# Two attention stages: the first tokens' output gated by halves, and ScalarE's high parts in another place

## What is computed

```python
q, k, v, f_logit, gate = _split(x @ w_in, [H * dh, H * dh, H * dh, H, D])
...
s = jnp.where(kpos[None, :] <= qpos[:, None], s, -jnp.inf)
p = jax.nn.softmax(s, axis=-1).astype(v.dtype)
return jnp.einsum('bhqs,bshd->bqhd', p, v)
...
return (jax.nn.silu(gate) * o.reshape(B, S, D)) @ w_out
```

## Time and profile before

| | us |
|---|---|
| median of 3 runs (1339.82 to 1340.50) | 1340.21 |
| the profiled execution's own time | 1334.75 |
| its span in the trace | 1333.0 |
| TensorE busy | 1280.7 (96%) |
| VectorE busy | 873.1 (65%) |
| ScalarE busy | 613.0 (46%) |
| TensorE's mean granted clock, share of full speed | 0.987 |

### The profile page before, as it was taken

The page is one execution under the profiler, slowest core; times in us unless marked ns, Lnnn a source line. Parts: engine busy times, 40 slices in busy tenths (PEclk is TensorE's granted clock), DMA queues, the critical chain, the costliest instruction groups (busy, mean ns, idle before and its releaser), DMA issues.

```text
span 1333.0 us, 16476 instructions
## 1 busy us (share of the span) xinstructions
PE 1280.7 (96%) x6717; PEld 1085.8 (81%) x6717; DVE 873.1 (65%) x1302; ACT 613.0 (46%) x838; POOL 24.1 (2%) x37
## 2 busy tenths in 40 slices
PE   6999999989999999999999988999999999999987
PEld 5888888978888888878888875778888899988876
DVE  6655557786655557685856668675555575667885
ACT  6444436525444445543544456554444443535361
POOL 2000000200000000000000000000000000000000
PEclk9999999999999999999999999999999999999899
DMA  9655545434655655456565340166555685346201
GB/s 305 223 189 184 186 152 181 160 127 143 205 189 189 189 190 172 155 179 222 188 198 181 102 158 1 46 207 190 189 190 169 118 234 165 130 163 217 96 1 63
DMA packets 158810, 218.16 MB, mean 164 GB/s; under 512 B 8256, under 2 KB 110992, under 8 KB 158736
## 3 DMA queue, kind: packets, MB, share of 16 engines
q1 hardware_dynamic: 156880, 212.56, 50.2%
q0 software_dynamic: 1376, 3.71, 0.9%
q10 hardware_dynamic: 480, 0.85, 0.2%
HBM read 216.04 MB, written 1.05 MB: 163 GB/s over the span
## 4 chain that ended last, share of the span: by engine, by line
PE 87%; DVE 7%; ACT 3%; issue 2%; DMA 1%; SPq 0%; DVEq 0%
PE PS L679 24%; PE PS L682 24%; PE PS L680 24%; PE PS L714 2%; PE PS L715 2%; PE PS L800 1%; ACT whi L1490 1%; PE PS L721 1%; DVE wlo L2010 1%; PE PS L992 1%; PE PS L699 1%; DMA raw<-in_ffn_w_in_dram 1%; PE PS L1275 1%; PE PS L1261 1%; PE PS L1288 1%
## 5 line engine op out<-in xcount | busy, mean ns | idle before, releaser
L2010 DVE TENSOR_TENSOR wlo<-raw,whi 128x2048 fp32r<-128x2048 f32 (+4 forms) x206 | 457.5, 2231 | 122.7 <-ACT whi L1490 121.9
L1490 ACT ACTIVATE whi<-raw 128x2048 fp32r<-128x2048 f32 (+4 forms) x206 | 381.4, 1864 | 64.4 <-DMA raw<-in_fox_w_in_dram 33.8
L679 PE MATMUL PS<-whi,XL 128*128 128x512 f32 (+3 forms) x992 | 385.4, 389 | 9.1 <-DVE XL L2057 3.5
L680 PE MATMUL PS<-wlo,XH 128*128 128x512 f32 (+3 forms) x992 | 379.3, 383 | 0.0
L682 PE MATMUL PS<-whi,XH 128*128 128x512 f32 (+3 forms) x992 | 264.6, 384 | 0.0
L679 PEld LDWEIGHTS PS<-whi,XL 128*128 128x128 f32 x992 | 187.1, 189 | 44.3 <-issue 3.9
L680 PEld LDWEIGHTS PS<-wlo,XH 128*128 128x128 f32 x992 | 187.2, 189 | 32.7
L682 PEld LDWEIGHTS PS<-whi,XH 128*128 128x128 f32 x992 | 185.1, 189 | 35.0
L1544 ACT ACTIVATE scr<-PS,rn 128x256 f32<-128x256 f32 x88 | 41.7, 474 | 227.0 <-PE PS L682 223.9
L679 PE MATMUL PS<-whi,GL 128*128 128x512 f32 x320 | 125.6, 392 | 0.0
L680 PE MATMUL PS<-wlo,GH 128*128 128x512 f32 x320 | 124.7, 390 | 0.0
(11 more groups left out here) (375 smaller groups left out, 1349.6 us busy)
## 6 DMA issues: line engine op xcount, KB each, us to landing
raw<-in_ffn_w_in_dram SPq DMA_DIRECT2D x174, 512.0 KB, 5.0
raw<-in_ffn_w_out_dram SPq DMA_DIRECT2D x88, 512.0 KB, 5.0
raw<-in_fox_w_in_dram SPq DMA_DIRECT2D x24, 512.0 KB, 8.2
raw<-in_a_w_in_dram SPq DMA_DIRECT2D x16, 512.0 KB, 4.6
raw<-in_dsa_w_in_dram SPq DMA_DIRECT2D x16, 512.0 KB, 5.9
raw<-in_kv_w_dram SPq DMA_DIRECT2D x12, 512.0 KB, 4.3
raw<-in_fox_w_in_dram SPq DMA_DIRECT2D x12, 344.0 KB, 5.2
raw<-in_a_w_out_dram SPq DMA_DIRECT2D x8, 512.0 KB, 4.5
```

The costliest lines, as they stand in the source:

```text
L679: mm(o, xl, wh, start=start and i == 0, stop=False, skip_group_check=True)
L680: mm(o, xh, wl, start=False, stop=False, skip_group_check=True)
L1490: A(whi[:, p % SLOTS, 0:n], raw[:, p % SLOTS, 0:n], ACT.Copy).then_inc(hi_done, 1)
L2010: V.tensor_tensor(wlo[:, p % SLOTS, 0:n], raw[:, p % SLOTS, 0:n], whi[:, p % SLOTS, 0:n].bitcast(F32), ALU.subtract).then_inc(lo_done, 1)
```

## The change

Three things, in both stages unless said otherwise.

- The first tokens' output is multiplied with the gate one bank at a time: `raw_first` (heads 0 to 3, as soon as their values are there) and `raw_second` (heads 4 to 7, after the gate's second half). TensorE's `value(2)` waits for the first, on the new semaphore `z_half`, and `value(3)` for the second.
- The gate's second half is made in two instructions, `silu_first` after ScalarE's first sigmoid (new semaphore `sig_half`) and `silu_second` after its second; the call of `split_to` that stood ahead of it on VectorE goes (in `fox` one low part, in `dsa` one), and that low part is made by the next call, behind `low_of_z`. One copy of turned shares comes ahead of `raw_second`, the other behind.
- In `dsa` ScalarE makes two of the output projection's high parts (first + 13, first + 14) after the exponentials of unit 1, and the last (first + 15) between the high parts of the two z.

```diff
@@ attend_four (TensorE)
                 turn_p(3)
+                pe.wait_ge(z_half, zstage[stage])
+                value(2)
                 pe.wait_ge(z_raw, 2 * (zstage[stage] - 1) + 1)
-                value(2)
                 value(3)
@@ even_bank (ScalarE)
-                split_to(min(chunk_end(stage, c) + AHEAD, first_piece["dsa_out"] + (4 if c == 5 else 1))
+                split_to(min(chunk_end(stage, c) + AHEAD, first_piece["dsa_out"] + (3 if c == 5 else 1))
@@ silu_sigmoid (ScalarE)
-                A(f_gate[:, m:m + 2, :], two(o), ACT.Sigmoid)
+                A(f_gate[:, m:m + 2, :], two(o), ACT.Sigmoid).then_inc(sig_half, 1)
@@ dsa (ScalarE)
             exps_four("dsa", 1)
+            split_to(first + 15)
             first_of_pt("dsa", 0)
...
             dsa_parts(0, 0)
+            split_to(NP)
             dsa_parts(1, 0)
@@ VectorE
+            def silu_first(stage, c, m, n):
+
+                dve.wait_ge(sig_half, n)
+                g = f_gate[:, m:m + 2, :]
+                V.tensor_tensor(g, g, two(bank_of(stage, c, 0)), ALU.mult)
+
+            def silu_second(stage, c, m):
+
+                dve.wait_ge(chunk_act, first_chunk[stage] + c + 1)
+                g = f_gate[:, m + 2:m + 4, :]
+                V.tensor_tensor(g, g, two(bank_of(stage, c, 1)), ALU.mult).then_inc(chunk_dve, 1)
+
...
+            def raw_first(stage):
+
+                dve.wait_ge(pv_done, unit0[stage] + 1)
+                V.tensor_tensor(z_mix[:, 0:4, :], O_ps[:, 0:4, :], f_gate[:, 0:4, 0:P], ALU.mult).then_inc(z_half, 1)
+
+            def raw_second(stage):
+
+                dve.wait_ge(pv_done, unit0[stage] + 2)
+                dve.wait_ge(chunk_dve, first_chunk[stage] + len(stages[stage][1]))
+                V.tensor_tensor(z_mix[:, 4:8, :], O_ps[:, 4:8, :], f_gate[:, 4:8, 0:P], ALU.mult).then_inc(z_raw, 1)
+
@@ fox (VectorE)
             scale_four("fox", 3)
-            silu_gate("fox", 8, 4)
-            dve.wait_ge(pv_done, unit0["fox"] + 2)
-            raw_z("fox", 0)
+            raw_first("fox")
+            silu_first("fox", 8, 4, 2)
+            silu_second("fox", 8, 4)
             second_of_pt("fox", 2)
+            raw_second("fox")
             second_of_pt("fox", 3)
@@ dsa (VectorE)
             scale_four("dsa", 3)
-            split_to(first + 14)
-            silu_gate("dsa", 5, 4)
-            dve.wait_ge(pv_done, unit0["dsa"] + 2)
-            raw_z("dsa", 0)
+            raw_first("dsa")
+            silu_first("dsa", 5, 4, 4)
+            silu_second("dsa", 5, 4)
             second_of_pt("dsa", 2)
+            raw_second("dsa")
             second_of_pt("dsa", 3)
```

More of the change, by code:

```diff
@@ L351, in program @@
         z_raw = sem("z_raw")
+        z_half = sem("z_half")
+        sig_half = sem("sig_half")
         z_hi = sem("z_hi")
```

## The result

The changed kernel took 1326.71 us (median of five). Runs of the kernel before taken on the same chip had a median of 1339.82 us. The ratio is **0.9921, with a 95% interval of 0.9893 to 0.9949** (the quotient of the two medians, 0.9902, lies in it too). The kernel is faster by about 0.8%, and the interval leaves out 1. On the 1340.21 us of before the ratio makes it 1329.6 us; forecast were 1330.9, and 1327.0 to 1334.2 as the range. The profiled execution took 1325.15 us with a span of 1323.1; 1325.4 was forecast for it.

A forecast was written before the change was run, and what follows sets the result against it. TensorE, 87% of the chain, was taken to bound the kernel, so only its waits and slowing count. 1.87 + 5.22 + 2.27 = 9.36 us off the median 1340.21 gave 1330.9, range 1327.0 to 1334.2.

The forecast's parts named there:

- First stage, 1.87: In fox, TensorE's value products begin at 1164.65 instead of 1166.52, 1.87 us earlier, by gating and multiplying in halves.
- Second stage, 5.22: In dsa, the value products begin at 1291.58, 5.22 us earlier, with the chunk's end bounding instead of ScalarE.
- Values at full clock, 2.27: In dsa, TensorE idles 0.3 us instead of 5.56 and keeps its clock: values take 3.81 instead of 6.08.
- High parts: In dsa, two of three fit ScalarE's 4.44 us gap, taking 3.61 with 0.8 to spare; 5.41 leaves the path.
- Just in time: In dsa, VectorE finishes the output's first half and first gating half by 1290.02 or 1290.11, before the second sigmoid at 1290.16.
- What is late next: After dsa's values: z and low parts in time; the last norm waits 3 us for parameters, hidden by half a microsecond.
- A: Rival: TensorE's last values run at half clock in spite of the short gap; gain 7.1, time 1333.1; 10%.
- B: Rival: the clock fall at 1240 to 1248 (3.4 us) moves; unmet 1327.5 (10%), a further one met 1334.3 (8%).
- C: Rival: the first stage's gain is eaten before dsa's index work ends, by transfers or parameter loads; 1332.7; 5%.
- D: Rival: TensorE's values are really held by something the change leaves alone, so all stays at 1340.2; 3%.
- E: Rival: a late transfer blocks ScalarE's high part in its dsa gap; slower, 1344 for a landing at 1292; 2%.
- The median: Whole kernel: the summed gain of 9.36 us taken off the median of 1340.21 gives 1330.9; 62%.

The follow-up runs named there:

- fox_only: Only the first stage's (fox) edit, on the kernel before; the second stage as before. Ratio 0.9982 (0.9959 to 1.0004).
- act_only: The kernel before with only ScalarE's high parts in dsa moved; VectorE and TensorE as before. Ratio 0.9971 (0.9952 to 0.999).
- low_back: The changed kernel with VectorE's low part in dsa put back ahead of the gating. Ratio 0.9941 (0.9919 to 0.9963).
- low_again: The kernel of low_back run once more, unchanged; the second stage's values took 5.33 us, against 5.44 in low_back.
- dsa_only: The kernel before with only the second stage (dsa) changed, on all three engines; fox as before. Ratio 0.9944 (0.9919 to 0.9969).
- three_again: Second run of the changed kernel with all three dsa high parts in ScalarE's gap ahead of the first turned shares. Ratio 0.9935 (0.9913 to 0.9958).
- halves_only: The changed kernel without the three edits that move ScalarE's high parts in dsa; both stages gated by halves. Ratio 0.996 (0.9938 to 0.9982).
- copy_first: The changed kernel with the copy of the first turned shares ahead of the second gating half, in both stages. Ratio 0.9932 (0.991 to 0.9954).

## Why the prediction was right

*First stage, 1.87.* Measured 1.86. *Second stage, 5.22.* Measured 5.21. *Values at full clock, 2.27.* Measured 2.27; but this term holds for the profiled execution of before alone. In fox_only the same gap (5.57 us) was followed by values of 5.49 us, by which the term would be 1.68. Within the terms, gating half, copy and issue were put at 0.645 + 0.645 + 0.13 = 1.42, and are 0.69 + 0.61 + 0.14 = 1.44 in the chain, and the sigmoid of the first stage began 0.19 us after the turnings, not 0.20. By that the forecast gives 2.25 from turnings to values, and 2.26 was measured, in both stages: these hundredths are the whole difference between 9.36 and 9.34. In VectorE's timeline a half lasts 0.68 to 0.69 us, and halves that follow one another start 0.60 us apart. The estimate from the Trainium skill (VectorE: DVE Perf Modes, the TRN2 errata), 0.66, stands between the two readings. Its call for large tiles pointed to a loss here; the extra per instruction is there (1.29 us for two halves, 1.23 for the whole), and is far less than what the halves save.

*High parts.* 3.61 us forecast with 0.8 to spare; 3.70 and 0.83. act_only shows that they and their order are worth 2.65 of the 5.21 without the rest (7.47 to 4.82).

*"Just in time."* The forecast had VectorE ready at 1290.02 to 1290.11 for 1290.16, so 0.05 to 0.14 us to spare; it had 0.22. low_back shows what the low part in front of it would cost: 1.87 us of idle time and 1.63 of clock.

*What is late next.* The norm's wait was put at 3 us, hidden by about half a microsecond. It is 3.09, with 0.71 to spare. No product waited for a low part or for the z between the two halves of the output; the waits of TensorE have no such line.

*The rivals.* A did not come. The forecast's argument against it, that the first stage ran at full speed after 2.21 us, is weaker than it looked: in low_back and low_again a gap of 2.2 us in the second stage was followed by half clock. With the change the idle time is 0.35 us, and in all five traces with 0.36 us or less there the values were made at full clock. B came in both directions: the fall at 1240 to 1248 was not met, which gave 2.7 us and not 3.4, and falls ahead of the first stage cost 2.06 more. C is excluded by fox_only's and dsa_only's T-end. D is excluded by T-V. E was not tried with a late transfer; three_again shows that ScalarE may come 0.87 us late to the turned shares and the exponentials still begin in time, as E's count had it.

*The median.* The range held. The point was 1.3 us above 1329.6. This rests on the ratio: the median as it stands, 1326.71, is 0.3 us below the range, and the kernel before had medians of 1335.8 to 1336.8 in the later comparisons, not 1340.2. The two ratios, 0.9921 and 0.9941, would be 10.6 and 7.9 us on 1340.2; 9.34 lies between and in both intervals.

## What to carry to other kernels

Chains that end at one wait must be shortened together, since to shorten one uncovers the other. In the second stage ScalarE's high parts alone took 2.65 us off T-V, VectorE's two remedies alone (halves_only) 1.74, and all together 5.21. Of VectorE's two, with the high parts moved, each alone gave 0.7 us and both gave 2.6. Idle time of TensorE ahead of short matmuls is paid twice when the clock falls (1.87 us of idle time and 1.63 of clock in low_back), so the last microseconds of a gap can be worth more than the first. And when a change of 0.7% is to be measured on a kernel whose executions differ by as much, measure from a fixed instruction ahead of the edit to the end: it gave each part to 0.1 us from one trace, where ten runs gave it to 3 us. Look at the granted clock behind that instruction too: the one trace with another fall there was 2.7 us off.

## What the runs showed of the hardware

The executions of the same instructions differ by 8.5 us before the first changed one. The first stage's turnings began anywhere from 1162.09 (act_only) to 1170.56 (copy_first) in the 13 executions compared here, and what differs is where the clock falls. The stretch 740 to 830, in the kernel before:

```profile
740.00:830.00 90.00, 80.37 (x513) 63.37 (x512) 64.63 (x124) 48.83 (x159) 0.00 (x0) 0.94 0.24 82
```

in fox_only, which came to its turnings at 1170.17:

```profile
740.00:830.00 90.00, 81.13 (x481) 64.56 (x481) 61.07 (x115) 46.99 (x148) 0.00 (x0) 0.89 0.25 88
```

in low_again, which came to them at 1162.63:

```profile
740.00:830.00 90.00, 80.36 (x533) 62.94 (x531) 67.63 (x125) 51.09 (x166) 0.00 (x0) 0.98 0.25 86
```

Nearly the same code had a granted clock of 0.89 to 0.98 there, with TensorE about equally busy. Added up over the stretches of 4 us from 24 to 1160 us (4 x (1 - clock)), the falls come to 6.8 to 15.4 us, and the start of the turnings less that sum is 1153.9 to 1155.8 in all 13: the scatter of 8.5 us shrinks to 1.9, so most of it is clock. Falls ahead of 24 us are left out of the sum: they come to 0 to 5.1 us, and yet at about 31 us the 13 executions lie within 1.3 us of each other. It fits what the Trainium skill says (TensorE: Matmul & The Clock Gate, What's actually happening), that the clock's windows run free of the kernel's start. Gaps behave differently by their length. After 2.90 to 5.57 us idle the fall came in all four executions (act_only, halves_only, before, fox_only). After 2.21 to 2.24 us it came in two of nine (low_back and low_again), and after 0.36 us or less in neither stage of any. Lengths as near as 2.23 and 2.21 don't make a limit; what tells these cases apart is open.
